# Two rings for the loads in place of one, in a two-block transformer kernel on one Trainium2 core

## Chip, cores and metric

One core of one Trainium2 chip. The metric is the device time of one execution in microseconds, the median of several runs. The program is one launch.

## What is computed

Two blocks on x (256 positions, 2048 channels, float32). The first block has two layers. Each multiplies x by `w_in` (2048 x 7680), runs four heads of differential attention, eight heads of dilated attention and a gated 31-tap convolution on slices of the result, gates them, multiplies by `w_out` and normalises (layer norm). The second block is conditioned by adaLN: `silu(c) @ w_mod + b_mod` gives six vectors of 2048 that shift, scale and gate; the same product with `c_ctx` gives the context's. It has an input projection, neighbourhood attention with context keys, a Fourier, a pooling and a short-convolution branch, gates, `w_o`, and a SwiGLU FFN of width 5632:

```
mod = jnp.split(jax.nn.silu(c) @ w_mod[i] + b_mod[i], N_MOD, axis=-1)
h = modulate(rms_norm(x, norm1_w[i]), sh1, sc1)
x = x + g1 * merge_branches(h, branches, w_gate[i], w_branch, w_o[i])
x = x + g2 * swiglu(modulate(rms_norm(x, norm2_w[i]), sh2, sc2), w_ffn_gate[i], w_ffn_up[i], w_ffn_down[i])
```

## The kernel before

All weights but w_mod are one stream of 888 chunks (`CHUNKS`), in the order in which they are used. A chunk is 128 x 1024 float32, 512 KB: two tiles of 128 rows by 512 columns. Each matmul in float32 is replaced by three on split operands: the weights and the activations are divided in a high part and a low part (`w_hi`, `w_lo`, `act_hi`, `act_lo`), and `products` (L864) issues high x high, high x low and low x high. A chunk so costs twelve matmuls (2 tiles, 2 blocks of 128 positions, 3 products).

The way of a chunk n:

- SP (`load`, L386) issues the DMA into one of four buffers of the ring `raw`, once that buffer is free.
- ScalarE (`split(n)`, L477 to L484) waits for the landing and for `chunk_used` of chunk n - 4, and copies it into `w_hi`, one of four buffers (`SPLIT`).
- VectorE (`split(n)`, L1280 to L1284) subtracts: `w_lo = raw - w_hi`, and raises `lo_ready`. After that the ring's buffer is free.
- PE (`chunk(n)`, L873) waits for `lo_ready` and multiplies, and raises `chunk_used`.

ScalarE and VectorE split chunk q + 4 in the step in which PE multiplies chunk q. Everything else they do (attention steps, convolution taps, evacuations, norms) is written out by hand between these splits, so the order of the work on each engine is fixed.

w_mod, turned, is a second stream, `mods`, of 192 chunks of the same size. VectorE multiplies an adaLN chunk by the row of silu(c) and sums along it (L1302); for the first 64 also by the row of silu(c_ctx) (L1300), the two operations one behind the other. The table `MODS_AFTER` (L116) says behind which weight chunk each adaLN chunk is used. In the two layers the gaps between uses are mostly 2, 3, 5 or 8 weight chunks; 11 of them are 2. From `Q_KV` on a use comes every third chunk, in the FFN every fourth, and none after about the FFN's first half.

Both streams go through the one ring. `load_order` (L138) merges them: weight chunk n, then the adaLN chunks used behind n. Entry e of this order waits for the use of entry e - 4, whichever kind it is.

SP issues all these loads from one queue, in order, and also the x rounds at the start. ScalarE's queue issues x, ctx (L665, L677) and other rows, POOL's queue the norm's rows (L445), the neighbourhood attention's bias rows (L447) and more.

Three passages are written so that PE need not stand at a norm: the end of layer 0 (`around_norm`, L1464, with `sum_tile` at L1446), the start of the FFN (`around_norm` with `branch_tile` at L1830), and between them the turn of the gated branches into layer 1's output projection (product at L1621, transposes at L892). At the two norms the last four chunks are multiplied by tile of positions, the next four chunks are split into buffers of their own (`AHEAD`, the tensors ahead_early and ahead_a to ahead_d), and `around_norm` interleaves the norm's serial chain with two of these splits: the second ahead chunk's low half stands just before the first step of the chain at the end of layer 0, and so it does at the FFN.

Of the kernel before, what the change touches and what calls it, by code (L numbers as in the profile page):

```python
# [8 lines left out]
F32 = mybir.dt.float32  # L9
F32R = mybir.dt.float32r  # L10
ALU = mybir.AluOpType
ACT = mybir.ActivationFunctionType
AX_X = mybir.AxisListType.X

P = 128
# [5 lines left out]
CH = 2 * COLS  # L21
# [19 lines left out]

RAW, SPLIT = 4, 4
IN_SLOTS, OUT_SLOTS = 15, 4
SLOTS = IN_SLOTS + OUT_SLOTS
LAYER = 8 * SLOTS
# [7 lines left out]
CHUNKS = Q_FF + FF * 24  # L55
# [60 lines left out]
def mods_after():  # L116
    after = {}
    m = 0
    for layer in range(DEPTH):
        for s in range(SLOTS):  # L120
            for c in MODS_OF_LAYER[layer].get(s, ()):
                after.setdefault(layer * LAYER + 8 * s + c + SPLIT, []).append(m)
                m += 1
    assert m == 2 * CTX_BLOCKS, m
    for i in range(6 * KT):
        after.setdefault(Q_KV + 16 + 3 * i, []).append(m)
        m += 1
    for i in range(2 * KT):
        after.setdefault(Q_FF + 16 + 4 * i, []).append(m)
        m += 1  # L130
    assert m == 2 * MOD_BLOCKS
    return after


MODS_AFTER = mods_after()


def load_order():  # L138
    order = []
    for n in range(CHUNKS):  # L140
        order.append((False, n))
        order.extend((True, m) for m in MODS_AFTER.get(n, ()))
    return order


LOADS = load_order()
ENTRY = {load: e for e, load in enumerate(LOADS)}


def is_ahead(n):  # L150
# [3 lines left out]
def last_user(n):  # L154

    return n - SPLIT - TAIL if is_ahead(n) or is_ahead(n - SPLIT) else n - SPLIT
# [13 lines left out]
def build(nc, stream, mods, c_rows, x_in, x_cols, ctx_cols, consts, vecs, lam_rows, rel_rows, ctx_in, ln_gb, conv_pw, cs_dft, inv_cnt, w_pool,  # L170
          na_rows, g_rows, out):
    with ExitStack() as ctx:
        def sb(name, shape, dt=F32):
            return ctx.enter_context(nc.sbuf_tensor(name, shape, dt))

        def sem(name):
            return ctx.enter_context(nc.semaphore(name))
# [4 lines left out]
        br_hi = sb("br_hi", [P, 4, S], F32R)  # L182
        br_lo = sb("br_lo", [P, 4, S], F32R)
        raw = sb("raw", [P, RAW, CH])
        w_hi = sb("w_hi", [P, SPLIT, CH], F32R)
        w_lo = sb("w_lo", [P, SPLIT, CH], F32R)
        act_hi = sb("act_hi", [P, KT, S], F32R)
# [2 lines left out]
        c_row = sb("c_row", [P, D])  # L190
# [51 lines left out]
        gflat = gtmp[:, :, :].rearrange("p t c -> p (t c)")  # L242
# [29 lines left out]
        def tiles_of(n):  # L272

            for first in AHEAD:
                if first <= n < first + TAIL:
                    both = ahead_at[first][n - first]
                    return both[:, 0:CH], both[:, CH:2 * CH]
            return w_hi[:, n % SPLIT, :], w_lo[:, n % SPLIT, :]
# [27 lines left out]
            return ps[:, b * COLS:(b + 2) * COLS].rearrange("p (j t) -> p j t", j=4)  # L306

        landed = [sem(f"landed{i}") for i in range(RAW)]
        hi_ready, lo_ready, chunk_used, mod_used = sem("hi_ready"), sem("lo_ready"), sem("chunk_used"), sem("mod_used")
        x_landed = [sem(f"x_landed{i}") for i in range(8)]  # L310
        first_landed, first_hi, first_lo, zeroed = sem("first_landed"), sem("first_hi"), sem("first_lo"), sem("zeroed")
# [71 lines left out]

        @block.sync
        def _(sp):
            def load(e):  # L386
                is_mod, i = LOADS[e]
                if e >= RAW:
                    was_mod, before = LOADS[e - RAW]
                    sp.wait_ge(mod_used if was_mod else lo_ready, before + 1)  # L390
                sp.dma_start(raw[:, e % RAW, :], (mods if is_mod else stream)[i]).then_inc(landed[e % RAW], 16)

            def load_x(r):
                sp.dma_start(x_stage[:, r], x_cols[r].rearrange("p (k t) -> p k t", k=2)).then_inc(x_landed[r], 16)

            sp.dma_start(raw[:, 0, 0:COLS], stream[0][:, 0:COLS]).then_inc(first_landed, 16)
            load_x(0)
            sp.dma_start(raw[:, 0, COLS:CH], stream[0][:, COLS:CH]).then_inc(landed[0], 16)
            for r in range(1, 4):
                load_x(r)  # L400
                load(r)
            for r in range(4, 8):
                load_x(r)
                if r == 5:
                    sp.dma_start(lam_in, bass.AP(lam_rows.tensor, 0, [[0, P], [1, DEPTH * 256]])).then_inc(consts_landed, 16)
                if r == 6:
                    sp.dma_start(C[:, P:], consts[:, P:]).then_inc(consts_landed, 16)
                if r == 7:
                    sp.dma_start(V[:, :], vecs).then_inc(consts_landed, 16)
                load(r)  # L410
            for e in range(8, len(LOADS)):
                load(e)
            for n in range(3):
                cols = slice(n * COLS, (n + 1) * COLS)
                sp.wait_ge(out_ready, n + 1)
                sp.dma_start(out[:, cols].rearrange("(t p) c -> p t c", p=P), x[:, :, cols]).then_inc(stored, 16)
            for t in range(TT):
                sp.wait_ge(out_ready, 4 + t)
                sp.dma_start(out[t * P:(t + 1) * P, 3 * COLS:], x[:, t, 3 * COLS:]).then_inc(stored, 16)
            sp.wait_ge(stored, 16 * 5)  # L420
# [55 lines left out]
        def _(act):  # L476
            def split(n):  # L477
                if n >= CHUNKS:
                    return
                e = ENTRY[False, n]  # L480
                act.wait_ge(landed[e % RAW], 16 * (e // RAW + 1))
                if n >= SPLIT:
                    act.wait_ge(chunk_used, last_user(n) + 1)
                nc.scalar.activation(tiles_of(n)[0], raw[:, e % RAW, :], ACT.Copy).then_inc(hi_ready, 1)  # L484

            def turn(first, r, b, k_round=None):

# [109 lines left out]
            for r in range(4):  # L597
                if r == 0:
                    act.wait_ge(first_landed, 16)
                    nc.scalar.activation(w_hi[:, 0, 0:COLS], raw[:, 0, 0:COLS], ACT.Copy).then_inc(first_hi, 1)  # L600
                    x_round(0)
                    act.wait_ge(landed[0], 16)
                    nc.scalar.activation(w_hi[:, 0, COLS:CH], raw[:, 0, COLS:CH], ACT.Copy).then_inc(hi_ready, 1)
                else:
                    x_round(r)
                    split(r)

            for layer in range(DEPTH):
                for s in range(SLOTS):
                    g = layer * SLOTS + s  # L610
                    for c in range(8):
# [4 lines left out]
                        if layer == 0 and s == 0 and c < 4:  # L616
                            x_round(4 + c)
                        split(q + SPLIT)
                        if layer == 1 and s == 0 and c < 4:
                            turn_both(TURN_LN, 4 + c)  # L620
# [40 lines left out]
                        if layer == 1:  # L661
# [10 lines left out]
                            if s == IN_SLOTS and 4 <= c <= 7:  # L672
# [3 lines left out]
                                i = c - 4  # L676
# [138 lines left out]
            for i in range(4):  # L815
                for c in range(4):
                    split(Q_NAP + 4 * i + c + SPLIT)
                    if i >= 1 and c in (1, 2):
                        k = 2 * (i - 1) + c - 1
# [457 lines left out]
        def _(dve):  # L1277
            ch = Chain(dve, dve_chain)

            def split(n):  # L1280
                if n < CHUNKS:
                    dve.wait_ge(hi_ready, n + 1)
                    hi, lo = tiles_of(n)
                    nc.vector.tensor_tensor(lo, raw[:, ENTRY[False, n] % RAW, :], hi.bitcast(F32), ALU.subtract).then_inc(lo_ready, 1)  # L1284

            def mods_of(n):


                for m in MODS_AFTER.get(n, ()):
                    e = ENTRY[True, m]  # L1290
                    j = e % RAW
                    block_n, h = divmod(m, 2)
                    k = slice(h * CH, (h + 1) * CH)
                    if m == 0:
                        dve.wait_ge(crow_ready, 2)
                    dve.wait_ge(landed[j], 16 * (e // RAW + 1))
                    if block_n < CTX_BLOCKS:
                        if m:
                            dve.wait_ge(mod_used, m)
                        nc.vector.scalar_tensor_tensor(gflat, raw[:, j, :], 1.0, ctx_row[:, k], ALU.mult, ALU.mult,  # L1300
                                                       accum_out=macc_ctx[:, block_n, h:h + 1])
                    nc.vector.scalar_tensor_tensor(raw[:, j, :], raw[:, j, :], 1.0, c_row[:, k], ALU.mult, ALU.mult,  # L1302
                                                   accum_out=macc[:, block_n, h:h + 1]).then_inc(mod_used, 1)

            def add_mods(lo, hi):
# [217 lines left out]
            for layer in range(DEPTH):  # L1523
                for s in range(SLOTS):
                    g = layer * SLOTS + s
                    for c in range(8):
# [22 lines left out]
                        if layer == 0 and s == 1:  # L1549
                            if c == 0:  # L1550
                                dve.wait_ge(lam_exp, 1)
                                e = lam[:, 4:8].rearrange("p (l two) -> p l two", two=2)
# [6 lines left out]
                            if c in (5, 6, 7):  # L1559

                                i = c - 5
# [21 lines left out]
                        if s == S_CONV:  # L1583
# [18 lines left out]
                            if c in (3, 5):  # L1602
                                i = c // 2 - 1
# [36 lines left out]
                        if layer == 1 and s == SLOTS - 1:  # L1640
# [7 lines left out]
                            if 1 <= c <= 7:  # L1648
                                ctx_round(c - 1)
                        mods_of(q + SPLIT)  # L1650

            for n in range(4):
# [20 lines left out]
            for n in range(11):  # L1673
                for c in range(8):
# [21 lines left out]
                    if n == 8 and c in (1, 3, 5, 7):  # L1696
# [5 lines left out]
                        for k in range(w + 1):  # L1702
                            half_w, lo, hi = 2 ** k // 2, 2 ** k, 273 - 2 ** k
# [8 lines left out]
                    if n == 10:  # L1712
# [5 lines left out]
                        if 3 <= c <= 5:  # L1718
                            k = c - 3
# [87 lines left out]
            for i in range(4):  # L1807
                for c in range(4):
                    q = Q_NAP + 4 * i + c
                    n = Y2_ORDER[2 * i] // 2  # L1810
# [8 lines left out]
                    if i >= 1 and c in (1, 2):  # L1819
                        k = 2 * (i - 1) + c - 1  # L1820
# [62 lines left out]
            for f in range(FF):  # L1883
                for s in range(16 if f == 0 else 24):
# [11 lines left out]
                    if s >= 16 and s % 2:  # L1896
                        n = (s - 16) // 2
# [195 lines left out]
```

## Time and profile before

| | |
|---|---|
| median of 3 runs | 2591.19 us (2591.19 to 2591.93) |
| the profiled execution | 2591.83 us, of it span 2590.0 us |
| PE busy | 2578.9 us, 11776 matmuls and transposes |
| VectorE busy | 1847.5 us |
| ScalarE busy | 1268.6 us |
| granted TensorE clock | 0.999 |
| DMA | 595.03 MB, mean 230 GB/s |

The profile page lists busy time per engine, the groups of instructions with the idle time before them and what ended it, and the DMA issues with their time to landing. The trace behind it can be asked for a stretch of time, for an engine or for who waited for whom. "SPq" is the queue of SP, which issues loads; "PEld" is PE's loading of its stationary operand, which runs beside the matmuls. Names such as ahead_early are the kernel's tensors.

### The profile page before, as it was taken

Reading aid. Unit: us, or ns where it says so; the run is one execution under the profiler, and the core shown is the slowest. Engines: PE = TensorE matmul, PEld = TensorE weight load, DVE = VectorE, ACT = ScalarE, POOL = GpSimd, SP = SyncE. Lnnn points to the kernel's source line nnn. Section 1 sums busy time; section 2 is a strip of 40 time slices with the busy share of each in tenths; the row PEclk is TensorE's granted clock in tenths of the full one; section 3 lists DMA queues with packets and bytes.
Section 4 is the critical chain, followed back from the end, with each engine's and each line's share of the span. In section 5 each row is a group of like instructions: output and inputs, shape, how many; then the busy total and the mean of one; then the engine's idle time right before and its main releaser. Section 6 shows DMA issues by size and latency. Waiting matters only on the chain.

```text
span 2590.0 us, 29986 instructions
## 1 busy us (share of the span) xinstructions
PE 2578.9 (100%) x11776; PEld 2134.5 (82%) x11776; DVE 1847.5 (71%) x2246; ACT 1268.6 (49%) x1590; POOL 33.3 (1%) x37
## 2 busy tenths in 40 slices
PE   9999999999999999999999999999999999999999
PEld 7888888888888888888888888888788888888887
DVE  6888878888887886566766766677656666655557
ACT  6455544645554467544555544444544444444443
POOL 0000000000000000010000000000000000000000
PEclk9999999999999999999999999999999999999999
DMA  8866568686667767878766667777567777756554
GB/s 325 274 213 204 187 235 258 199 267 203 211 194 266 271 213 258 256 256 254 235 214 223 219 230 260 259 251 236 172 230 239 237 241 238 224 191 205 193 189 161
DMA packets 163932, 595.03 MB, mean 230 GB/s; under 512 B 18096, under 2 KB 18256, under 8 KB 162384
## 3 DMA queue, kind: packets, MB, share of 16 engines
q1 hardware_dynamic: 158352, 571.41, 67.0%
q0 software_dynamic: 2352, 11.67, 1.2%
q10 hardware_dynamic: 3088, 10.04, 1.1%
q8 instruction: 93, 1.52, 0.2%
q14 instruction: 47, 0.39, 0.1%
HBM read 590.94 MB, written 2.11 MB: 229 GB/s over the span
## 4 chain that ended last, share of the span: by engine, by line
PE 97%; DVE 2%; DMA 1%; ACT 0%; issue 0%; POOL 0%; DVEq 0%; ACTq 0%
PE ps L868 31%; PE ps L870 31%; PE ps L869 30%; PE ps L892 1%; PE ps L960 1%; DMA raw<-weights 1%; PE ps L1148 1%; DVE w_lo L1284 0%; PE ps L976 0%; PE ps L986 0%; PE ps L995 0%; PE ps L1142 0%; PE ps L985 0%; PE ps L1122 0%; PE ps L1004 0%
## 5 line engine op out<-in xcount | busy, mean ns | idle before, releaser
L1284 DVE TENSOR_TENSOR w_lo<-raw,w_hi 128x1024 fp32r<-128x1024 f32 x879 | 1073.2, 1224 | 686.1 <-ACT w_hi L484 684.2
L484 ACT ACTIVATE w_hi<-raw 128x1024 fp32r<-128x1024 f32 x879 | 930.5, 1060 | 1281.4 <-PE ps L870 1185.4
L868 PE MATMUL ps<-w_hi,act_hi 128*128 128x512 f32 x3104 | 1224.6, 395 | 2.7 <-DVE act_lo L1311 1.9
L870 PE MATMUL ps<-w_hi,act_lo 128*128 128x512 f32 x3104 | 1210.3, 390 | 0.0
L869 PE MATMUL ps<-w_lo,act_hi 128*128 128x512 f32 x3104 | 1208.7, 389 | 0.0
L868 PEld LDWEIGHTS ps<-w_hi,act_hi 128*128 128x128 f32 x3104 | 583.3, 188 | 124.2 <-issue 5.5
L870 PEld LDWEIGHTS ps<-w_hi,act_lo 128*128 128x128 f32 x3104 | 582.9, 188 | 123.3
L869 PEld LDWEIGHTS ps<-w_lo,act_hi 128*128 128x128 f32 x3104 | 583.6, 188 | 117.6
L1302 DVE SCALAR_TENSOR_TENSOR raw<-raw,c_row 128x1024 f32<-128x1024 f32 x192 | 233.9, 1218 | 0.0
L868 PE MATMUL ps<-w_hi,br_hi 128*128 128x512 f32 x416 | 162.6, 391 | 0.0
L869 PE MATMUL ps<-w_lo,br_hi 128*128 128x512 f32 x416 | 161.9, 389 | 0.0
L870 PE MATMUL ps<-w_hi,br_lo 128*128 128x512 f32 x416 | 161.8, 389 | 0.0
L1354 DVE SCALAR_TENSOR_TENSOR shared<-conv_pad,vecs_sb,shared 128x256 f32<-128x256 f32 x240 | 99.9, 478 | 0.0
L870 PEld LDWEIGHTS ps<-w_hi,br_lo 128*128 128x128 f32 x416 | 78.1, 188 | 16.3
L869 PEld LDWEIGHTS ps<-w_lo,br_hi 128*128 128x128 f32 x416 | 78.1, 188 | 15.9
L868 PEld LDWEIGHTS ps<-w_hi,br_hi 128*128 128x128 f32 x416 | 78.1, 188 | 15.9
L1300 DVE SCALAR_TENSOR_TENSOR gtmp<-raw,ctx_row 128x1024 f32<-128x1024 f32 x64 | 78.0, 1218 | 1.7 <-DMA raw<-mods 1.5
L544 ACT ACTIVATE flat<-ps 128x1024 f32<-128x1024 f32 x45 | 45.8, 1019 | 0.1
L1903 DVE TENSOR_TENSOR flat<-flat,ps 128x1024 f32<-128x1024 f32 x36 | 43.7, 1214 | 0.0
L430 POOL TENSOR_TENSOR rstd<-ms,half 128x2 f32<-128x2 f32 (+3 forms) x12 | 21.0, 1753 | 1276.4 <-DVE ms L1842 341.1
L561 ACT ACTIVATE head<-head,small 128x128 f32<-128x128 f32 (+1 forms) x64 | 28.2, 441 | 0.0
L892 PEld LDWEIGHTS ps<-consts_sb,flat 128*128 128x128 f32 x144 | 17.8, 139 | 6.3 <-DVE flat L1621 1.8
(292 smaller groups left out, 1141.6 us busy)
## 6 DMA issues: line engine op xcount, KB each, us to landing
raw<-weights SPq DMA_DIRECT2D x887, 512.0 KB, 4.2
raw<-mods SPq DMA_DIRECT2D x192, 512.0 KB, 4.5
flat<-ln_gb POOLq DMA_DIRECT2D x4, 1024.0 KB, 7.3
flat<-x_cols SPq DMA_DIRECT2D x8, 256.0 KB, 6.5
flat<-conv_pw POOLq DMA_DIRECT2D x8, 256.0 KB, 5.2
x<-x_in ACTq DMA_DIRECT2D x4, 512.0 KB, 5.6
flat<-ctx_in ACTq DMA_DIRECT2D x1, 2048.0 KB, 8.5
shared<-na_rows POOLq DMA_DIRECT2D x2, 1024.0 KB, 9.7
```

Of the source, the lines that this page charges most:

```text
L484: nc.scalar.activation(tiles_of(n)[0], raw[:, e % RAW, :], ACT.Copy).then_inc(hi_ready, 1)
L544: nc.scalar.activation(dst, pair(group_bank(g)), func).then_inc(freed_a, 1)
L561: ins = nc.scalar.activation(p, p, ACT.Exp, bias=nm[:, n:n + 1], scale=A_SCALE if two else HEAD_SCALE, accum_out=sums[:, n:n + 1])
L868: nc.tensor.matmul(acc, xh, wh, start=first, stop=False)
L869: nc.tensor.matmul(acc, xh, wl, start=False, stop=False)
L870: mm = nc.tensor.matmul(acc, xl, wh, start=False, stop=last)
L892: mm = nc.tensor.transpose(bank(b, at, at + P), src(t, k0 + k), ident)
L1284: nc.vector.tensor_tensor(lo, raw[:, ENTRY[False, n] % RAW, :], hi.bitcast(F32), ALU.subtract).then_inc(lo_ready, 1)
L1300: nc.vector.scalar_tensor_tensor(gflat, raw[:, j, :], 1.0, ctx_row[:, k], ALU.mult, ALU.mult, accum_out=macc_ctx[:, block_n, h:h + 1])
L1302: nc.vector.scalar_tensor_tensor(raw[:, j, :], raw[:, j, :], 1.0, c_row[:, k], ALU.mult, ALU.mult, accum_out=macc[:, block_n, h:h + 1]).th ...
L1354: ins = nc.vector.scalar_tensor_tensor(conv_acc[:, j, :], conv_pad[:, j, k:k + S], w, conv_acc[:, j, :], ALU.mult, ALU.add)
L1903: nc.vector.tensor_tensor(p2[:, :, cols], p2[:, :, cols], pair(4 if n % 2 else 6), ALU.add).then_inc(acc_done, 1)
```

## The change

`raw` gets three buffers and holds weight chunks only. A fourth buffer of the same size, `mod_raw`, holds the adaLN chunks, one at a time, with a semaphore of its own for its landings. Weight chunk n waits for the low half of chunk n - 3. An adaLN chunk waits for the use of the one before it; it is issued right after weight chunk u + 3, where u is the chunk behind which the one before it is used (the first after weight chunk 8). The operations on ScalarE and VectorE are the same and in the same order.

```diff
-RAW, SPLIT = 4, 4
+RAW, SPLIT, MOD_RAW = 3, 4, 1
...
-def load_order():
-    order = []
-    for n in range(CHUNKS):
-        order.append((False, n))
-        order.extend((True, m) for m in MODS_AFTER.get(n, ()))
-    return order
-
-
-LOADS = load_order()
-ENTRY = {load: e for e, load in enumerate(LOADS)}
+def mod_loads():
+
+
+    users = [n for n in sorted(MODS_AFTER) for _ in MODS_AFTER[n]]
+    return [8] * MOD_RAW + [min(max(8, n + RAW), CHUNKS - 1) for n in users[:-MOD_RAW]]
+
+
+MOD_LOADS = mod_loads()
...
         raw = sb("raw", [P, RAW, CH])
+        mod_raw = sb("mod_raw", [P, MOD_RAW, CH])
...
         landed = [sem(f"landed{i}") for i in range(RAW)]
+        mod_landed = [sem(f"mod_landed{i}") for i in range(MOD_RAW)]
...
-            def load(e):
-                is_mod, i = LOADS[e]
-                if e >= RAW:
-                    was_mod, before = LOADS[e - RAW]
-                    sp.wait_ge(mod_used if was_mod else lo_ready, before + 1)
-                sp.dma_start(raw[:, e % RAW, :], (mods if is_mod else stream)[i]).then_inc(landed[e % RAW], 16)
+            def load(n):
+                if n >= RAW:
+                    sp.wait_ge(lo_ready, n - RAW + 1)
+                sp.dma_start(raw[:, n % RAW, :], stream[n]).then_inc(landed[n % RAW], 16)
...
-            for e in range(8, len(LOADS)):
-                load(e)
+            m = 0
+
+            def load_mods(n):
+
+                nonlocal m
+                for _ in range(MOD_LOADS.count(n)):
+                    if m >= MOD_RAW:
+                        sp.wait_ge(mod_used, m - MOD_RAW + 1)
+                    sp.dma_start(mod_raw[:, m % MOD_RAW, :], mods[m]).then_inc(mod_landed[m % MOD_RAW], 16)
+                    m += 1
+
+            for n in range(8, CHUNKS):
+                load(n)
+                load_mods(n)
...
-                e = ENTRY[False, n]
-                act.wait_ge(landed[e % RAW], 16 * (e // RAW + 1))
+                act.wait_ge(landed[n % RAW], 16 * (n // RAW + 1))
...
                 for m in MODS_AFTER.get(n, ()):
-                    e = ENTRY[True, m]
-                    j = e % RAW
...
-                    dve.wait_ge(landed[j], 16 * (e // RAW + 1))
+                    dve.wait_ge(mod_landed[m % MOD_RAW], 16 * (m // MOD_RAW + 1))
...
-                    nc.vector.scalar_tensor_tensor(raw[:, j, :], raw[:, j, :], 1.0, c_row[:, k], ALU.mult, ALU.mult,
+                    nc.vector.scalar_tensor_tensor(mod_raw[:, m % MOD_RAW, :], mod_raw[:, m % MOD_RAW, :], 1.0, c_row[:, k], ALU.mult, ALU.mult,
                                                    accum_out=macc[:, block_n, h:h + 1]).then_inc(mod_used, 1)
```

## Rows read from the trace of the kernel before

**Rows 1.** The page: the span and PE's busy time.

```profile
span 2590.0 us, 29986 instructions
...
PE 2578.9 (100%) x11776; PEld 2134.5 (82%) x11776; DVE 1847.5 (71%) x2246; ACT 1268.6 (49%) x1590; POOL 33.3 (1%) x37
```

**Rows 2.** The page's costliest groups: out<-in, count | busy, mean ns | idle before, releaser.

```profile
L1284 DVE TENSOR_TENSOR w_lo<-raw,w_hi 128x1024 fp32r<-128x1024 f32 x879 | 1073.2, 1224 | 686.1 <-ACT w_hi L484 684.2
L484 ACT ACTIVATE w_hi<-raw 128x1024 fp32r<-128x1024 f32 x879 | 930.5, 1060 | 1281.4 <-PE ps L870 1185.4
```

**Rows 3.** PE's timeline, a chunk's first matmuls and the next's: start, us, what.

```profile
832.38 0.39 PE L868 MATMUL ps<-w_hi,act_hi 128*128 128x512 f32 x1
832.61 0.39 PE L869 MATMUL ps<-w_lo,act_hi 128*128 128x512 f32 x1
...
835.10 0.39 PE L868 MATMUL ps<-w_hi,act_hi 128*128 128x512 f32 x1
```

**Rows 4.** Waits of SP's queue: us in total, times, longest us.

```profile
SPq L391 <- DVE w_lo L1284: 1882.6, 875, 6.4
SPq L391 <- DVE raw L1302: 275.0, 192, 4.3
```

**Rows 5.** The page's DMA issues: count, KB each, median us to landing.

```profile
raw<-weights SPq DMA_DIRECT2D x887, 512.0 KB, 4.2
raw<-mods SPq DMA_DIRECT2D x192, 512.0 KB, 4.5
```

**Rows 6.** Windows, three stretches: length, busy us of each engine, clock, DMA share, GB/s.

```profile
449.00:470.00 21.00, 20.57 (x97) 16.21 (x96) 16.16 (x26) 12.02 (x23) 1.24 (x2) 1.00 0.55 179
...
806.00:846.00 40.00, 38.63 (x186) 31.46 (x185) 26.00 (x31) 15.36 (x20) 1.65 (x3) 1.00 0.83 309
...
1835.00:1866.00 31.00, 29.53 (x140) 23.41 (x140) 22.14 (x35) 18.80 (x37) 1.25 (x2) 1.00 0.44 139
```

**Rows 7.** Timeline of the start: load 4's issue, and chunk 3's copy on ScalarE.

```profile
7.61 0.33 SPq L391 DMA_DIRECT2D raw<-weights  x1
...
12.04 1.06 ACT L484 ACTIVATE w_hi<-raw 128x1024 fp32r<-128x1024 f32 x1 [0.38 <-DMA raw<-weights]
```

**Rows 8.** VectorE's timeline: the end of one adaLN use, the start of the next.

```profile
88.58 0.08 DVE L1302 DVE_READ_ACCUMULATOR raw<-raw,c_row 128x1 f32 x1
...
91.02 1.22 DVE L1300 SCALAR_TENSOR_TENSOR gtmp<-raw,ctx_row 128x1024 f32<-128x1024 f32 x1
```

**Rows 9.** Timelines of ScalarE, VectorE and PE at the end of layer 0.

```profile
455.09 1.06 ACT L484 ACTIVATE ahead_early<-raw 128x1024 fp32r<-128x1024 f32 x1 [1.64 <-DMA raw<-weights]
456.64 1.06 ACT L484 ACTIVATE ahead_b<-raw 128x1024 fp32r<-128x1024 f32 x1 [0.49 <-DMA raw<-weights]
...
457.33 0.68 DVE L1446 SCALAR_TENSOR_TENSOR x<-x,ps 128x512 f32<-128x512 f32 x1
...
460.78 1.09 PE L899 MATMUL ps<-consts_sb,x 128*128 128x128 f32 x8
```

**Rows 10.** Chain of waits (first row) and timelines, start of layer 1's output projection.

```profile
825.06 10.36 DMA raw<-weights
...
830.70 1.23 DVE L1300 SCALAR_TENSOR_TENSOR gtmp<-raw,ctx_row 128x1024 f32<-128x1024 f32 x1 [1.54 <-DMA raw<-mods]
...
836.54 1.23 DVE L1284 TENSOR_TENSOR w_lo<-raw,w_hi 128x1024 fp32r<-128x1024 f32 x1 [3.46 <-ACT w_hi L484]
...
839.84 1.23 DVE L1284 TENSOR_TENSOR w_lo<-raw,w_hi 128x1024 fp32r<-128x1024 f32 x1 [0.34 <-ACT w_hi L484]
840.98 1.22 DVE L1621 TENSOR_TENSOR flat<-ps,flat 128x1024 f32<-128x1024 f32 x1
...
842.25 0.66 PE L892 MATMUL ps<-consts_sb,flat 128*128 128x128 f32 x4 [1.37 <-DVE flat L1621]
```

**Rows 11.** Timelines of ScalarE and VectorE at the start of the FFN.

```profile
1843.55 1.06 ACT L484 ACTIVATE ahead_c<-raw 128x1024 fp32r<-128x1024 f32 x1 [1.20 <-DMA raw<-weights]
...
1844.78 0.69 DVE L1830 TENSOR_TENSOR gtmp<-ps,flat 128x512 f32<-128x512 f32 x1 [0.79 <-PE ps L870]
```

More of the change, by code:

```diff
@@ L479, in split @@
                     return
-                e = ENTRY[False, n]
-                act.wait_ge(landed[e % RAW], 16 * (e // RAW + 1))
+                act.wait_ge(landed[n % RAW], 16 * (n // RAW + 1))
                 if n >= SPLIT:
                     act.wait_ge(chunk_used, last_user(n) + 1)
-                nc.scalar.activation(tiles_of(n)[0], raw[:, e % RAW, :], ACT.Copy).then_inc(hi_ready, 1)
+                nc.scalar.activation(tiles_of(n)[0], raw[:, n % RAW, :], ACT.Copy).then_inc(hi_ready, 1)
             def turn(first, r, b, k_round=None):
@@ L1283, in split @@
                     hi, lo = tiles_of(n)
-                    nc.vector.tensor_tensor(lo, raw[:, ENTRY[False, n] % RAW, :], hi.bitcast(F32), ALU.subtract).then_inc(lo_ready, 1)
+                    nc.vector.tensor_tensor(lo, raw[:, n % RAW, :], hi.bitcast(F32), ALU.subtract).then_inc(lo_ready, 1)
             def mods_of(n):
                 for m in MODS_AFTER.get(n, ()):
-                    e = ENTRY[True, m]
-                    j = e % RAW
                     block_n, h = divmod(m, 2)
@@ L1299, in mods_of @@
                             dve.wait_ge(mod_used, m)
-                        nc.vector.scalar_tensor_tensor(gflat, raw[:, j, :], 1.0, ctx_row[:, k], ALU.mult, ALU.mult,
+                        nc.vector.scalar_tensor_tensor(gflat, mod_raw[:, m % MOD_RAW, :], 1.0, ctx_row[:, k], ALU.mult, ALU.mult,
                                                        accum_out=macc_ctx[:, block_n, h:h + 1])
-                    nc.vector.scalar_tensor_tensor(raw[:, j, :], raw[:, j, :], 1.0, c_row[:, k], ALU.mult, ALU.mult,
+                    nc.vector.scalar_tensor_tensor(mod_raw[:, m % MOD_RAW, :], mod_raw[:, m % MOD_RAW, :], 1.0, c_row[:, k], ALU.mult, ALU.mult,
                                                    accum_out=macc[:, block_n, h:h + 1]).then_inc(mod_used, 1)
```

## The prediction

> **What bounds the kernel now.** The page first: TensorE (PE) is busy for 2578.9 of 2590.0 us, so almost nothing is left for it to gain by waiting less [rows 1]. In the groups by cost, VectorE's subtraction for the low halves (1.22 us each) and ScalarE's copy for the high halves (1.06 us each) are short, and most of ScalarE's idle time ends with a matmul: it waits for one of the four split buffers to come free [rows 2]. The PE timeline gives the pace of a weight chunk: the first matmul of one starts at 832.38, of the next at 835.10, so 2.72 us for twelve. Split chunks are normally three ahead of PE, 3 x 2.72 = 8.2 us, of which the two splits take 2.3: a spare of 5.9 us before a late chunk stops PE [rows 2, 3]. Then the load queue's own waits: all are waits for a ring buffer, 875 for a weight chunk's low half and 192 for an adaLN chunk, one for each adaLN load of the program [rows 4]. A chunk lands 4.2 us (weights) or 4.5 us (adaLN) after its issue, by the medians [rows 5]. Last the windows: PE's idle time sits in a few places. Three stretches, around the end of layer 0, the end of layer 1's input projection and the start of the FFN, lack 21.00 - 20.57 = 0.43, 40.00 - 38.63 = 1.37 and 31.00 - 29.53 = 1.47 us, together 3.27 us [rows 6].
>
> **The steady state.** After the change weight chunk n is issued when chunk n - 3 is split, not n - 4. One turn of a ring buffer is 4.2 + 1.06 + 1.22 = 6.5 us, and three chunks last 8.2 us: three buffers keep up, with 1.7 us over. Where an adaLN chunk is among the last four loads, the old ring held three weight chunks anyway (two where two adaLN chunks were near), so there the change is neutral or gives a buffer. The number of copies, subtractions, dot products, loads and waits is the same, each load still has one wait. Cost: 0. The cover is the 5.9 us above; without it a late chunk costs PE what it is late.
>
> **The first loads.** Load 3 now waits for chunk 0's low half, as load 4 did, so it goes out at 7.61, the time of load 4 before, and the x rounds behind it shift too. With the median 4.2 us it lands at 11.8; ScalarE took it at 12.04 [rows 5, 7]. Zero; at worst the later x rounds add 0.5 us, at best nothing.
>
> **The adaLN loads.** Chunk m is now issued once chunk m - 1 is used. The code's table has 11 uses that follow the last by only two weight chunks, all in the two layers, where a use is two operations of VectorE, 2.4 us. Row pattern: the one ends at 88.66, the next starts at 91.02 [rows 8]. Issued at 88.7 it lands at 93.2 by the median, so VectorE stands 2.2 us. On VectorE the split of the next chunk is queued behind that, and for it wait the low half, the next weight load and PE. In the queue of SP only the next weight load stands behind the wait, and that load waits for a later split of VectorE anyway, so SP loses nothing. Eight or nine such waits of 1.3 to 2.2 us come one at a time, and 5.9 us cover each. Cost: 0, between nothing and their whole length (about 16 us) if the cover were gone. The 128 later uses are three or more chunks apart and one operation long: 8.2 - 1.2 = 7.0 us for a load of 4.5. Nothing.
>
> **Place 1, end of layer 0.** Here the split of a weight chunk stands in VectorE's queue ahead of the layer norm's serial chain. Before, ScalarE got the second ahead chunk at 455.09, as soon as it landed, the third at 456.64, and the residual sum that starts the chain began at 457.33, right after the second one's low half. PE's transposes, which need the chain, began at 460.78 [rows 9]. In the changed order of loads an adaLN load takes the place of this chunk (the one whose user comes much later, but whose buffer is free), and each weight load moves one place back: the second ahead chunk gets the landing of the third, 1.55 us later. The chain starts 1.55 us later, and the transposes too, since they start as soon as the chain lets them. **+1.55 us**; between 0 (if the earlier transfers let it land sooner) and 2.5.
>
> **Place 2, start of layer 1's output projection.** ctx, the norm's rows and the bias rows are loaded here, and transfers are slow. Before, adaLN chunk 58 was issued first and used at 830.70 after a wait of 1.54 us; weight chunk 274 was issued behind it at 825.06 and took 10.36 us, and VectorE split it at 836.54. PE's transposes waited 1.37 us more, until 842.25, for the gate product that began at 840.98 [rows 10]. The two loads now change places, since 274 waits for chunk 271's low half and adaLN 58 for 57's use. If the queue keeps its order, 274 is there at 830.7 and adaLN 58 at 835.4. VectorE has 58's two operations (2.4) before 274's low half, which then starts at 837.8 and not 836.54: +1.26. A little comes back behind it: from 836.54 to the product at 840.98 are 4.44 us, which hold a wait of 0.34 us for ScalarE's copy, ready by then in the new order; 837.8 + 4.10 = 841.9. **+0.9 us**; from -1.4 (58 lands early, PE's wait goes) to +2.5.
> The Trainium skill bears on this ("DMA: Bandwidth & Descriptors", Queues, rings and completion order): descriptors of one ring are taken in order, but transfers may complete out of order. By the first half the sum above stands, by the second adaLN 58 could land before 835.4 and this term be -1.4, the total 1.15.
>
> **Place 3, start of the FFN.** No adaLN chunk is due here, so the old ring held four weight chunks and now holds three. Before, ScalarE got the third ahead chunk at 1843.55, when it landed; VectorE stood for 0.79 us before the branch sum at 1844.78, for PE; the FFN's first tile hangs on that sum and PE is short of work here, as the 1.47 us of its idle time in this stretch say [rows 6, 11]. With each load one place later, the second ahead chunk lands at 1843.5; copied by 1844.6 and subtracted by 1845.8, it delays the sum from 1844.78 to 1845.8. **+1.0 us**; from 0 to 2.
>
> **The tail.** In the last 45 us PE waits for VectorE, whose queue is full; chunks lie ready. Zero.
>
> **Sum.** 1.55 + 0.9 + 1.0 = 3.45 us. The profiled execution took 2591.83 us (span 2590.0), 0.64 above the median of the runs, 2591.19; so 2595.3 against its own time, and 2591.19 + 3.45 = 2594.6 us as a median. A measurement tells about 0.2% of this kernel, 5.2 us, from no change; the bounds are 2586.0 and 2596.4.
>
> **The rivals.** (a) Nothing shows: the loads land earlier than their places in line say, since VectorE's earlier idle time absorbs them. For it: in places 1 and 3 I read the landing of one load off the place in line of another. Time 2591.2. That the change does not do what it says belongs here: if loads were still issued as before, the same time.
> (b) A gain: loads that wait no longer for an adaLN use end PE's idle time in the three stretches. All of it is 3.27 us: 2587.9, still within 0.2%. For it, place 2's wait for chunk 274; against it, places 1 and 3 wait for a serial chain. The Trainium skill's rule speaks for more room ("Perfetto Trace Analysis", Identifying the Most-Contended Engine): headroom is to be judged by the weight loads' busy share, not the matmuls'. That share is 82% here, which would leave 18% or 466 us. Against that, matmuls start 0.227 us apart with every buffer full [rows 3], which no ring changes.
> (c) Slower beyond 0.2%: in place 2's slow transfers the ring of three does not close. At 8.5 us a turn is 10.8 us, 3.6 per chunk, 0.9 more than PE needs; it decides where transfers stay above 8.2 - 2.3 = 5.9 us for over 5.9 / 0.9 = 6.6 chunks running. For some 20 chunks of congestion that is 18 - 5.9 = 12 us: 2603. Against it: adaLN chunks are frequent there, so the old ring had three weight buffers there too, and PE lost only 1.37 us.
>
> **The numbers.** Forecast case 0.62 (of it 0.08 above 2596.4, if two places reach their upper bounds), (a) 0.18, (b) 0.06, (c) 0.12, and 0.02 for a gain that no case here explains. Slower: 0.08 + 0.12 = 0.20; faster: 0.02; the rest, 0.78, within 0.2%. The range goes from 2589.5 (half of the gain case) to 2600.0 (all upper bounds, 7.5 us, and a little of (c)).
>
> **What would show it.** PE's busy time stays at 2578.9 and its idle time grows by 3 us. The residual sum of place 1 begins at 458.9 and not 457.33; place 2 shows a VectorE wait for an adaLN load near 835 and none of ScalarE for chunk 274; place 3's sum begins at 1845.8, after a low half and not after PE. Elsewhere ScalarE's waits for weights become more, without a PE wait; about nine VectorE waits of 1.3 to 2.2 us for adaLN loads appear. The forecast is wrong if PE waits for a low half in a fourth place, or if SP's queue issues in another order than I worked out.

## The result and the profile after

The changed kernel takes 2610.99 us (median of 4 runs, 2607.96 to 2615.35), the kernel before 2591.53 beside it (4 runs, 2591.19 to 2591.93). The ratio is 1.0076 [1.0063, 1.0089]: slower by 19.5 us where 3.45 were forecast, and beyond the end of the range, 2600.0. The runs of the changed kernel also scatter by 7.4 us where those of before stay within 0.7.

The page of the changed kernel: the span, the engines, the chain that ended last, one group and two DMA issues. They answer to [rows 1, 2, 5].

```profile
span 2610.7 us, 29986 instructions
...
PE 2584.5 (99%) x11776; PEld 2136.2 (82%) x11776; DVE 1846.6 (71%) x2246; ACT 1268.5 (49%) x1590; POOL 34.2 (1%) x37
...
PE 86%; DVE 6%; DMA 5%; ACT 2%; issue 1%; POOL 0%; SPq 0%; ACTq 0%; DVEq 0%
...
L493 ACT ACTIVATE w_hi<-raw 128x1024 fp32r<-128x1024 f32 x879 | 930.5, 1060 | 1301.6 <-PE ps L879 1096.1
...
raw<-weights SPq DMA_DIRECT2D x887, 512.0 KB, 4.2
mod_raw<-mods SPq DMA_DIRECT2D x192, 512.0 KB, 4.5
```

Every engine has the same instructions and nearly the same busy time; the median landing times are those of [rows 5]. TensorE's idle time grew from 11.1 us (2590.0 - 2578.9) to 26.2 (2610.7 - 2584.5), and its busy time by 5.6. ScalarE waits for a split buffer 89 us less than in [rows 2]. What it waits for instead stands in the waits of the changed kernel (who, for whom: us in total, times, longest):

```profile
PE ps L877 <- DVE w_lo L1293: 5.1, 6, 1.4
PE ps L969 <- DVE flat L1579: 4.1, 2, 3.3
...
ACT w_hi L493 <- DMA raw<-weights: 205.5, 113, 5.7
...
DVE gtmp L1307 <- DMA mod_raw<-mods: 21.3, 10, 6.1
```

The kernel before has 95.9 us and 54 waits in the third row, 1.5 us and one wait in the fourth, and no PE wait for a low half at all.

Where the time went is read off the first matmul of a weight chunk, in both traces (us):

```
chunk     before     after    difference
   20      64.05     72.29       8.2
  100     307.46    317.49      10.0
  156     477.83    491.65      13.8
  196     589.22    607.49      18.3
  300     911.74    930.58      18.8
  887    2581.87   2602.54      20.7
```

8.2 us are lost in the first 20 chunks, 10.0 between chunks 20 and 196 (layer 0's end and layer 1's beginning), 0.6 around the output projection of place 2, 1.8 in the 587 chunks after that. The largest single steps are 4.0 at chunk 19 and 3.1 at chunk 152 (place 1); place 3 is 0.7, and the last two chunks are 1.1.

**The start.** The chain of waits of the changed kernel, 9 to 75 us (start, us, what):

```profile
7.18 5.02 DMA raw<-weights
...
12.23 1.07 ACT w_hi L493
...
13.32 1.24 DVE w_lo L1293
...
14.58 7.58 DMA raw<-weights
...
22.18 1.07 ACT w_hi L493
...
23.27 1.24 DVE w_lo L1293
...
24.53 4.96 DMA raw<-weights
...
31.85 7.67 DMA raw<-weights
...
41.89 6.75 DMA raw<-weights
```

TensorE isn't in it: up to 48.6 us the chain is the ring itself, load, copy, subtraction, and the load that the subtraction lets go. One turn carries three chunks and takes 7.40, 9.95, 7.32 and 10.04 us, 8.7 on average or 2.89 per chunk, where TensorE uses one in 2.72. A landing takes 5.0 to 7.7 us here, not the median 4.2. The kernel before has landings as long there (8.62 us for chunk 12), but one buffer more. The windows of the two kernels, before first (length, busy us of PE, PEld, DVE, ACT, POOL, granted clock, DMA share, GB/s), say why:

```profile
12.00:40.00 28.00, 28.00 (x126) 23.15 (x124) 18.48 (x25) 15.81 (x18) 0.00 (x0) 1.00 1.00 391
```

```profile
12.00:40.00 28.00, 28.00 (x123) 22.69 (x122) 15.38 (x17) 13.09 (x16) 0.00 (x0) 1.00 0.96 348
...
40.00:60.00 20.00, 17.56 (x75) 13.54 (x74) 11.52 (x15) 11.63 (x10) 0.00 (x0) 1.00 0.69 250
```

The 16 DMA engines are full or nearly so (shares 1.00 and 0.96). The kernel before has one load more in flight and gets more out of them, 391 against 348 GB/s; chunk 8 lands at 23.63 in place of 26.22, chunk 15 at 38.45 in place of 48.64. So it collects a spare of chunks and the changed kernel doesn't: chunk 15's low half is ready 5.58 us before PE takes it in the kernel before, and 0.05 us before in the changed one. PE's timeline of the changed kernel shows the end of it (in brackets the idle time before, and what ended it):

```profile
51.03 0.50 PE L877 MATMUL ps<-w_hi,act_hi 128*128 128x512 f32 x1 [0.62 <-DVE w_lo L1293]
...
55.30 0.47 PE L877 MATMUL ps<-w_hi,act_hi 128*128 128x512 f32 x1 [1.22 <-DVE w_lo L1293]
...
66.99 1.75 PE L969 MATMUL ps<-consts_sb,flat 128*128 128x128 f32 x8 [3.26 <-DVE flat L1579]
```

The largest of these waits, 3.26 us of the 4.0 that chunk 19 starts later, isn't for a chunk. ScalarE and VectorE do their work in a fixed order, so the late loads push everything else back too. VectorE's timeline of the changed kernel:

```profile
53.93 2.36 DVE L1293 TENSOR_TENSOR w_lo<-raw,w_hi 128x1024 fp32r<-128x1024 f32 x2 [2.95 <-ACT w_hi L493]
...
65.72 1.22 DVE L1579 TENSOR_TENSOR flat<-flat 128x1024 f32<-128x1024 f32 x1
```

Chunk 16 has landed at 50.11, but ScalarE's work on the row of c (L646, from 51.03) stands ahead of its copy, until 52.85; in the kernel before that work starts at 43.99, with split chunks to spare. VectorE has the pair of low halves at 53.93 and not 46.88, has almost no idle time from there on, and reaches the product `flat`, which PE's transposes wait for, at 65.72 and not 58.89.

**The adaLN waits.** VectorE's timeline of the changed kernel near the end of layer 0, and one use in place 2:

```profile
440.29 2.35 DVE L1293 TENSOR_TENSOR w_lo<-raw,w_hi 128x1024 fp32r<-128x1024 f32 x2
...
444.74 1.23 DVE L1307 SCALAR_TENSOR_TENSOR gtmp<-mod_raw,ctx_row 128x1024 f32<-128x1024 f32 x1 [2.10 <-DMA mod_raw<-mods]
...
450.49 1.23 DVE L1307 SCALAR_TENSOR_TENSOR gtmp<-mod_raw,ctx_row 128x1024 f32<-128x1024 f32 x1 [1.10 <-DMA mod_raw<-mods]
...
470.01 1.23 DVE L1293 TENSOR_TENSOR ahead_early<-raw,ahead_early 128x1024 fp32r<-128x1024 f32 x1 [3.29 <-ACT ahead_early L493]
471.16 0.68 DVE L1453 SCALAR_TENSOR_TENSOR x<-x,ps 128x512 f32<-128x512 f32 x1
...
853.51 1.23 DVE L1307 SCALAR_TENSOR_TENSOR gtmp<-mod_raw,ctx_row 128x1024 f32<-128x1024 f32 x1 [6.09 <-DMA mod_raw<-mods]
...
855.80 1.23 DVE L1293 TENSOR_TENSOR w_lo<-raw,w_hi 128x1024 fp32r<-128x1024 f32 x1
```

A use ends, its buffer's next load goes out, and VectorE stands before the next use, as predicted. But low halves are queued behind, each of them lets one weight load go, and these loads are late: then ScalarE waits for weights, and VectorE for ScalarE (470.01), right before the residual sum of place 1. (ScalarE's copy before 470.01 begins at 468.92. The profile puts its wait to PE, but its load goes out at 464.48 and lands at 468.90, so it is the load that it waits for.)

### The profile page after: what moved, and what is told of

Read it like the earlier page. It is cut to its first block, busy times and chain, and to the rows that moved or that the text cites. A ratio compares the mean times of both kernels' runs of the same rounds, so it can differ in the third digit from the quotient of the medians.

```text
span 2610.7 us, 29986 instructions
## 1 busy us (share of the span) xinstructions
PE 2584.5 (99%) x11776; PEld 2136.2 (82%) x11776; DVE 1846.6 (71%) x2246; ACT 1268.5 (49%) x1590; POOL 34.2 (1%) x37
## 3 DMA queue, kind: packets, MB, share of 16 engines
q10 hardware_dynamic: 3088, 10.04, 1.1%
## 4 chain that ended last, share of the span: by engine, by line
PE 86%; DVE 6%; DMA 5%; ACT 2%; issue 1%; POOL 0%; SPq 0%; ACTq 0%; DVEq 0%
PE ps L877 27%; PE ps L879 27%; PE ps L878 27%; DMA raw<-weights 4%; DVE w_lo L1293 2%; DMA mod_raw<-mods 1%; ACT w_hi L493 1%; DVE gtmp L1307 1%; DVE mod_raw L1309 1%; PE ps L901 1%; DVE shared L1361 1%; PE ps L1157 1%; PE ps L969 1%; PE ps L995 0%; PE ps L985 0%
## 5 line engine op out<-in xcount | busy, mean ns | idle before, releaser
L1309 DVE SCALAR_TENSOR_TENSOR mod_raw<-mod_raw,c_row 128x1024 f32<-128x1024 f32 x192 | 234.0, 1219 | 0.0
L1307 DVE SCALAR_TENSOR_TENSOR gtmp<-mod_raw,ctx_row 128x1024 f32<-128x1024 f32 x64 | 78.1, 1220 | 21.5 <-DMA mod_raw<-mods 21.3
L969 PE MATMUL ps<-consts_sb,flat 128*128 128x128 f32 x144 | 19.2, 280 | 4.1 <-DVE flat L1579 4.1
## 6 DMA issues: line engine op xcount, KB each, us to landing
shared<-na_rows POOLq DMA_DIRECT2D x2, 1024.0 KB, 10.2
```

Source lines behind the costliest of these rows:

```text
L969: mm = nc.tensor.transpose(bank(b + j // 2, at, at + P), src(t, j), ident)
L1307: nc.vector.scalar_tensor_tensor(gflat, mod_raw[:, m % MOD_RAW, :], 1.0, ctx_row[:, k], ALU.mult, ALU.mult, accum_out=macc_ctx[:, block_n, ...
L1309: nc.vector.scalar_tensor_tensor(mod_raw[:, m % MOD_RAW, :], mod_raw[:, m % MOD_RAW, :], 1.0, c_row[:, k], ALU.mult, ALU.mult, accum_out=m ...
```

## The experiments

Two causes seemed possible after this: the three weight buffers, or the single adaLN buffer. Each ratio below is to the kernel before, timed beside it; losses by chunk come from one trace each. Room for a fifth buffer of 4 KB per partition comes from four small tiles moved into an unused part of a tile of constants, which leaves the 29986 instructions as they are.

**Four weight buffers and one for adaLN** (`e_raw4`)

```diff
-RAW, SPLIT, MOD_RAW = 3, 4, 1
+RAW, SPLIT, MOD_RAW = 4, 4, 1
-        rstd = sb("rstd", [P, 48])
+        rstd = C[:, 320:368]
...
```

> The changed kernel with a fourth weight buffer (five buffers in all); the small tensors rstd, ss, q_scale and g_row move into a dead part of consts_sb to make room. Theory W (the missing weight buffer costs PE at the start, where transfers are saturated, about 8 us, and the single adaLN buffer costs the other 12 us): about 2603 us, PE stalls before 70 us gone, VectorE's waits for adaLN loads of about 20 us still there. Rival M (the single adaLN buffer alone, the start is chance): 2611 us less little. Rival R (the weight ring alone): 2591 us, like before.

Measured: 2596.0 us, ratio 1.0016 [1.0007, 1.0026]. Of the 19.5 us, 15 are gone, more than theory W allowed, while VectorE waits for adaLN nearly as before the edit (18.3 us in 10 waits) and ScalarE for weights only 26.3 us. 4.0 us are still lost by chunk 20, and 0.7 after it.

**Three weight buffers and two for adaLN** (`e_mod2`; `MOD_RAW` 2, the same tiles moved)

> The changed kernel with two adaLN buffers (three weight buffers, five in all), small tensors moved as in e_raw4. Theory W: VectorE's waits for adaLN loads fall from 21 us to under 4, the losses after 100 us go (about 12 us), the start's 8 us stay: about 2599 us. Rival M: 2591 us. Rival R: 2611 us.

Measured: 2604.07 us, 1.0048 [1.0033, 1.0063]. VectorE no longer waits for adaLN at all, ScalarE still for weights: 166.5 us in 90 waits. 7.6 us are lost by chunk 20, 2.2 more by chunk 156, nothing more by chunk 196, and 2.2 behind it. None of the three theories gave these two numbers. Three weight buffers cost something whatever adaLN has; a single adaLN buffer costs much beside three weight buffers (12.4 us behind chunk 20, against 4.4 with two) and little beside four (0.7).

**Four weight buffers for the first 16 chunks only** (`e_start`). The adaLN buffer is lent to the weights there, and the first adaLN load waits until chunk 15 is split:

```diff
+MOD_LOADS[0] = 18
+FOUR = 16
...
+def place(n):
+    return n % 4 if n < FOUR else (n - FOUR) % 3
...
+def frees(n):
+    return n - 4 if n < FOUR + 3 else n - 3
...
-                if n >= RAW:
-                    sp.wait_ge(lo_ready, n - RAW + 1)
+                if frees(n) >= 0:
+                    sp.wait_ge(lo_ready, frees(n) + 1)
...
+                    else:
+                        sp.wait_ge(lo_ready, FOUR)
...
```

> The changed kernel, four buffers, but the idle adaLN buffer serves as the fourth weight buffer for chunks 0 to 15; from chunk 16 three weight buffers as in the changed kernel, and the first adaLN load goes out once chunk 15 is split. Theory W: the start's 8 us come back and nothing else: 2603 us, PE at chunk 20 near 64 us and not 72. Rival M: 2611 us. Rival R: between, since the rest of the program keeps three buffers.

Measured: 2604.37 us, 1.0048 [1.0032, 1.0065]. Chunk 20 is at 63.62 us, 0.4 earlier than in the kernel before: the whole loss of the start is gone, by the fourth buffer and the held back adaLN load together. The loss after it isn't: +4.7 at chunk 100, +8.3 at 156, +10.4 at 196. The same window as above in this kernel:

```profile
12.00:40.00 28.00, 28.00 (x125) 23.18 (x124) 19.21 (x25) 15.82 (x18) 0.00 (x0) 1.00 1.00 394
```

**adaLN uses at least three weight chunks apart** (`e_gap3`). Only the table is changed (the slots of both layers; layer 1's exceptions alike):

```diff
-MODS_OF_SLOT = {0: (7,), 1: (2, 4, 7), 2: (1, 5), 3: (2, 4, 7), 4: (2, 4, 7), 13: (4, 6), 14: (3, 7), 15: (3, 6),
-                16: (1, 3, 5), 17: (1, 3, 5)}
+MODS_OF_SLOT = {0: (7,), 1: (2, 4, 7), 2: (1, 5), 3: (1, 4, 7), 4: (2, 5), 13: (3, 6), 14: (2, 5), 15: (0, 3, 6),
+                16: (1, 4, 7), 17: (2, 5)}
...
+MODS_OF_SLOT[5] = (0, 7)
...
```

> The changed kernel with the table of adaLN uses changed so that none of the first 64 follows the last by fewer than three weight chunks (11 did by two); the number of uses and of loads is the same. Theory W: the loop from one use over the next load to the next use (2.4 + about 4.5 us, 6.9 in all) fits in three chunks (8.2 us) and not in two (5.4 us); VectorE's waits for adaLN loads go down to a few us and about 8 to 12 us come back: 2599 to 2603 us. Rival R: 2611 us, no change.

Measured: 2603.12 us, 1.0047 [1.0032, 1.0062]. VectorE's waits for adaLN fall from 21.3 to 3.9 us. The start is worse (10.7 us at chunk 20); behind it only 3.4 us are lost up to the end, where the changed kernel loses 12.4.

**The control: the same table in the kernel before** (`e_bgap3`)

> The kernel before (one shared ring of four) with the table of e_gap3 alone, a control. The table only matters where a buffer holds nothing but adaLN chunks: 2591 us, no change; if it unloads VectorE in general, up to 3 us faster (2588 us).

Measured: 2591.6 us, 1.0000 [0.9991, 1.0010]. The table alone is worth nothing to the kernel before.

**Both together** (`e_both`): four buffers at the start, and the table

> Four buffers in all: the start's repair of e_start and the table of e_gap3 together. In the first e_start had lost nothing at chunk 20 and e_gap3 lost 3.4 us behind it; if the two causes are separate, 3 us behind before: 2594 us. If each repair only moves the same loss, 2600 us or more.

Measured: 2596.93 us, 1.0021 [1.0011, 1.0031]. The expectation had 2594 for two separate causes and 2600 for one that only moves; it is between them. Most of the loss goes, not all: from 0.9 us ahead at chunk 20 it falls to 6.8 behind at chunk 887, in small steps (2.3 at chunk 43, 1.2 at 152, five more of 0.5 to 1.0). ScalarE still waits 197.9 us for weights.

**The first adaLN load later.** In the changed kernel it goes out at 22.18 us, inside the full DMA stretch, for a use at 59.90; in the kernel before at 43.96, for a use at 53.19. With four weight buffers it goes out at 16.89.

```diff
+MOD_LOADS[0] = 18
```

Alone, with three weight buffers (`e_late0`):

> The changed kernel (three weight buffers, one for adaLN) with the first adaLN load issued behind weight load 18 instead of 8, about where the kernel before issued it. Theory P (an early adaLN load takes 1.3 us of a saturated DMA start, and its use of the queue is most of the start's loss): PE at chunk 20 within 2 us of before, 2604 us. Theory W (the third buffer is most of it): PE at chunk 20 still 6 to 7 us late, 2609 us.

Measured: 2609.62 us, 1.0072 [1.0056, 1.0087]. Chunk 20 is at +7.2 us, 1.0 better. With four weight buffers (`e_raw4_late`):

> Four weight buffers and one for adaLN as in e_raw4, and the first adaLN load behind weight load 18. e_raw4 was 4.0 us behind at chunk 20 though it had the fourth weight buffer; theory P+W says the early adaLN load is that rest: PE at chunk 20 level with before, 2592 us in all (the waits for adaLN loads of 18 us stay and cost under 1 us with a fourth weight buffer behind them). If the rest was something else (the order of the x rounds): 2596 us as e_raw4.

Measured: 2591.86 us, 1.0001 [0.9992, 1.0010]: the kernel before. So the 4 us that four weight buffers had left at the start were this load. The waits of this kernel:

```profile
DVE gtmp L1308 <- DMA mod_raw<-mods: 17.6, 10, 6.2
...
ACT w_hi L494 <- DMA raw<-weights: 16.9, 14, 4.6
```

VectorE stands ten times and 17.6 us for adaLN, nearly as in the changed kernel, up to 6.2 us at a time, and it costs little: behind the start the kernel loses 0.5 us against the kernel before.

**The row load moved** (`e_lam`). Chunk 5's landing is 2.65 us later than before, right behind the load of the lambda rows. This kernel loads them behind chunk 7:

```diff
-                if r == 5:
-                    sp.dma_start(lam_in, ...)
...
+            sp.dma_start(lam_in, ...)
```

> The changed kernel with the load of lam_in (one 2 KB row of HBM read by all 128 partitions, 256 KB), which stood in SP's queue between the loads of chunks 4 and 5, moved behind the load of chunk 7. In the changed kernel it landed 6.6 us after its issue and chunk 5 behind it at 19.44, while the kernel before had it hidden in a longer backlog. If this one slow load starts the loss: chunk 5 lands near 17 us, PE's spare at chunks 5 to 7 is 2 us and more instead of 0.2, and the loss at chunk 20 falls from 8 us to about 5: 2608 us. If the ring of three alone makes the loss: chunk 20 as late as before, 2611 us, only chunk 5 lands earlier.

Measured: 2609.91 us, 1.0077 [1.0060, 1.0094]. Chunk 5 lands at 16.53 and not 19.44, and chunk 20 still starts 8.0 us late. This transfer isn't the cause; of the two that were moved, row and adaLN load, neither returns more than 1.0 us of the start's loss while there are three weight buffers.

**Versions that might beat both**: four weight buffers, the late load and the table (`e_raw4_late_gap3`); and one shared ring of five with the table (`e_ring5_gap3`)

> Five buffers: four for weights, one for adaLN, first adaLN load behind weight load 18, and the table of e_gap3. e_raw4_late was level with before, with 17.6 us of VectorE waits for adaLN loads. If these waits cost nothing but the 0.7 us at the output projection of layer 1: 2591 us with the waits under 4 us. If they hold PE up in small amounts everywhere: 2588 us.

> The shared ring of the kernel before with five buffers, and the table of e_gap3; the small tensors moved. A ring deeper than four has little left to give: PE's idle time outside the start is 3 to 5 us, most of it in serial chains of the norms. 2590 to 2591 us; if late loads still cost PE anything, down to 2588 us.

Measured: 2589.28 us, 0.9993 [0.9983, 1.0002], and 2590.08, 0.9994 [0.9985, 1.0004]. In the trace of the first, 2.8 us are won, 0.9 of them by chunk 20 already, where the control's trace is 0.7 ahead too; the interval does not separate either from the kernel before.

What is lost or won between chunk 20 and chunk 887 (us, the difference to the kernel before, less that at chunk 20):

```
                                          table as it is    uses 3 apart
three weight buffers                           +12.4            +3.4
three, and two for adaLN                        +4.4
three, but four for the first 16 chunks        +13.2            +7.7
four weight buffers                             +0.7
four weight buffers, late first adaLN load      +0.5            -1.9
```

Four weight buffers nearly bear the late adaLN loads; three don't. With four and the late load the table returns 2.4 us (from 0.5 behind to 1.9 ahead), all at chunks 274 and 275 (place 2), where VectorE stood 6.2 us for adaLN; 0.5 of it comes in the control's trace too.

With three, the single traces give the table 9.0 and 5.5 us. That difference isn't to be explained, since the traces scatter: the late load alone and the moved row alone, with the same three buffers and table, lose 10.2 and 8.8 us behind chunk 20 where the changed kernel loses 12.4. The medians of the runs are surer. Against the kernel before beside them, the changed kernel is 19.5 us behind, and 11.9 with the table; with four buffers for the first 16 chunks it is 13.1 behind, and 5.4 with the table. So the table returns 7.6 and 7.7 us, the same in both; the intervals of these figures are 3 to 4 us each way. With hardly an adaLN wait left, a ring of three loses 3.4, 4.4 and 7.7 us behind chunk 20 in three traces.

## Why the prediction was wrong

**The first loads: this step failed.** I said "Zero; at worst the later x rounds add 0.5 us"; it is 8.2 us. The issue itself was right (load 3 at 7.18 us, landed at 12.21). But I priced one load, with a median over 887, which says nothing of the first 20: those on the chain take 5.0 to 7.7 us. A turn is then 8.7 us on average, more than the 8.2 that TensorE needs for three chunks, and nothing in it makes up for a late load: the delay goes into the next turn. And "a spare of 5.9 us" was read where chunks were three ahead. There it is about right (5.6 us, the median of chunks 300 to 600, in both kernels), but at the start it has yet to be built. There was also a term missing: the change issues the first adaLN load at 22.18 us and not 43.96. Shown by the versions with four buffers: the fourth one alone returns 4.2 of the 8.2 us, the later adaLN load on top of it the rest; the later load alone returns 1.0.

**The adaLN loads: near in number, wrong in price.** "Eight or nine such waits of 1.3 to 2.2 us" were ten: six of 1.3 to 2.5, three of 0.8 to 1.1, and one of 6.1 us, 21.3 in all. The step that failed is "come one at a time, and 5.9 us cover each. Cost: 0". The bound given for lost cover, about 16 us, holds the 7.6 us that the table brings with three weight buffers by the medians. With four the kernel with the same waits is 0.5 us behind the kernel before, so the pricing was nearly that of the ring of four, which is the one that the change takes away. With three, the loads behind a wait go out late, and the spare is smaller when the next wait comes, two to eight chunks later: between chunks 156 and 190 a low half is ready 3.3 us before PE takes it (median), 4.9 in the kernel before. That the two rings cover for each other, and that the change shortens both, was in no rival.

**The steady state: right where no adaLN chunk waits.** From chunk 300 to 885, two thirds of the program, the loss is 0.7 us, and all of it is place 3's.

**The tail: 1.1 us, priced at zero.** It is lost at chunks 886 and 887, where PE waits 0.8 us for VectorE's `flat` (L1929). The kernel with four buffers only at the start, whose ring is the same there, loses nothing at these chunks, so the cause stays open.

**Place 1: about right, but buried.** Predicted +1.55; the step at chunk 152 is 3.1. Where the adaLN waits are gone (the table, or the second adaLN buffer) it is 1.1 and 1.25. With four weight buffers and the late load it is below 0.2, though the order of loads is swapped there too (with four and the early load it is 1.1, of which 0.7 are back by chunk 155). So the swap that I gave as the cause costs little where there are four weight buffers. In the changed kernel an ahead chunk comes later still (the 3.29 us of the timeline above).

**Place 2: right in the order of loads, near in the sum.** Predicted +0.9; measured +1.0 at chunk 274, where PE waits 0.93 us for this chunk's low half, and -0.4 at 275, where its wait for the gate product falls from 1.37 to 0.94 us: together +0.6. It is +1.1 and -0.4 with four weight buffers and the late load, and -0.1 and -1.7 with the table besides. The loads changed places as worked out: chunk 274 landed first, at 848.86, the adaLN chunk 4.6 us behind it at 853.49 (4.7 predicted), with the VectorE wait of 6.09 us. ScalarE's wait for chunk 274 fell from 7.66 to 2.83 us; it was predicted gone, and 4.34 us for the next chunk are new. For the order of landings I had left two cases open. None of the 1097 transfers on SP's queue landed before one issued ahead of it, in either trace: the first case. The Trainium skill allows transfers of one ring to complete out of order ("DMA: Bandwidth & Descriptors", Queues, rings and completion order); no run here shows that for loads of this size.

**Place 3: right.** Predicted +1.0, and a branch sum that follows a low half and not PE. Measured +0.7; VectorE's timeline of the changed kernel:

```profile
1863.20 1.23 DVE L1293 TENSOR_TENSOR ahead_b<-raw,ahead_b 128x1024 fp32r<-128x1024 f32 x1 [1.08 <-ACT ahead_b L493]
1864.34 0.68 DVE L1837 TENSOR_TENSOR gtmp<-ps,flat 128x512 f32<-128x512 f32 x1
```

**The rivals.** (c) had half of the mechanism: a ring of three that doesn't close under slow transfers, 3.6 us per chunk at 8.5 us landings. I placed it in place 2 and argued it down there, rightly (0.6 us net from chunk 196 to 300). It lay at the start, where the DMA share is 1.00 from 12 to 40 us, in the trace of before already. The 18% of headroom that (b) took from the weight loads' busy share showed nowhere: the share is 82% in both kernels, and the best version wins 2.8 us. And the sign against the forecast came: PE waits for a low half outside the three places (before 41.92, 51.03 and 55.30 us), and its busy time, which was to stay, grew by 5.6 us.

**Open.** Of the four buffers at the start with the table, what lies behind the steps that add up to 7.7 us wasn't followed. Which of the start's other transfers (rows, constants, context) fill the DMA engines wasn't tried apart. That the scatter of the changed kernel comes from its standing open to every late landing is argued, not shown. So is the way from one adaLN wait to the next: what is shown is that it costs with three weight buffers and hardly with four.

## What to carry to other kernels

Size a ring by the landing time of the busiest stretch, not by the median of the program, and carry a delay round the ring: buffers x pace of the consumer must exceed landing + processing (here 3 x 2.72 = 8.2 us against a turn of 8.7), or the loss grows with each turn. A spare is something built up under good conditions; read it in the stretch where you want to spend it, and in the kernel after the change, since the spare that hid one part of a change may be what the other part removes. A load given a buffer of its own can go out much earlier than it used to (here 22.18 us and not 43.96): look at what it then competes with. And where a version is slower by some us, compare medians of runs before explaining the difference of two traces.

## What the runs showed of the hardware

**The clock after a stall.** The windows of the changed kernel behind two stalls of TensorE (3.26 us before 66.99, 1.69 us before 602.17):

```profile
68.00:72.00 4.00, 4.00 (x15) 3.30 (x14) 3.50 (x6) 1.81 (x2) 2.30 (x4) 0.66 0.85 265
602.00:608.00 6.00, 5.83 (x23) 4.46 (x24) 5.73 (x11) 1.32 (x3) 0.00 (x0) 0.72 0.74 229
```

The seventh figure is the granted clock: 0.66 and 0.72, that is partly at 1.2 GHz in place of 2.4. Matmuls there start 0.43 us apart and not 0.227, and it costs 1.06 us at chunk 20 and 1.6 at chunk 196, on top of the waits. The kernel before is at 1.00 in both windows and in [rows 6]. This is a part of the 5.6 us by which PE's busy time grew, and I had not priced it: a stall of some us can cost more than itself. `e_start` shows it a third time: 2.41 us of idle time before 130.30, granted 0.66 from 131 to 136 us, 1.6 us lost at chunk 44.

**One row takes as long as a chunk.** The load of the lambda rows, one row copied to 128 partitions, took 6.6 us from issue to landing (11.53 to 18.13) in the full stretch, and chunk 5, issued behind it, landed behind it at 19.44. In the kernel before it took 7.0 us, but behind a backlog that hid it: it landed 0.8 us after the load ahead of it, where in the changed kernel it landed 3.4 us after. What such a load delays so depends on what is in flight ahead of it.
